# The last products of the PEER mixer, turned over: feature-major sums in PSUM in place of token-major ones

## The reference

```python
def chunk(args):
    xc, ec, gc = args
    ug = u[ec]
    act = jax.nn.gelu(jnp.einsum('td,thkd->thk', xc, ug), approximate=False)
    return jnp.einsum('thk,thkd->td', gc * act, v[ec])
...
x = x + (1.0 + gt2[:, None, :]) * peer_ffn(h, ...)
```

## Time and profile before

| | |
|---|---|
| median of 3 runs | 3288.6 us |
| the profiled execution | 3290.19 us, of which the span of its instructions is 3288.4 us |
| TensorE busy (matmul / weight load) | 90% / 81% of the span |
| VectorE, ScalarE, GpSimd busy | 70%, 34%, 3% |
| granted TensorE clock, mean | 0.954 of 2.4 GHz |
| scores stage of layer 0, layer 1 | about 808 to 1257.9, 2439 to 2890.1 us |
| mix stage of layer 0, layer 1 | about 1257.9 to 1620.5, 2890.1 to 3253.8 us |

### The profile page before, as it was taken

How to read it: one execution, slowest core, us unless ns; L and a number is a source line. 1 busy time by engine, 2 the same in 40 slices (tenths; PEclk the granted TensorE clock), 3 DMA queues, 4 the chain that set the end, 5 groups by cost and what they waited for, 6 DMA issues and landing times. The chain is left out here.

```text
span 3288.4 us, 49870 instructions
## 1 busy us (share of the span) xinstructions
PE 2962.9 (90%) x19180; PEld 2662.7 (81%) x19180; DVE 2314.4 (70%) x4571; ACT 1114.9 (34%) x1532; POOL 99.0 (3%) x120
## 2 busy tenths in 40 slices
PE   4997898879999999999769879897899999999996
PEld 4996787768999998887569858776789999988885
DVE  6888564545887847888578895645468868478885
ACT  3434321201444444333234342211024444433332
POOL 0000003200000000000000000031000000000000
PEclk8998999989999999999979989998999999999998
DMA  6552340053666688887465424300546575978783
GB/s 243 184 188 77 119 170 8 29 208 116 207 208 213 215 295 283 283 280 277 142 238 188 156 77 159 129 8 32 211 139 213 189 249 190 320 266 284 278 281 109
DMA packets 268992, 613.57 MB, mean 187 GB/s; under 512 B 45520, under 2 KB 210000, under 8 KB 211664
## 3 DMA queue, kind: packets, MB, share of 16 engines
q1 hardware_dynamic: 203152, 576.79, 49.9%
q10 hardware_dynamic: 65600, 33.55, 3.4%
HBM read 540.53 MB, written 69.73 MB: 186 GB/s over the span
## 5 line engine op out<-in xcount | busy, mean ns | idle before, releaser
L835 PE MATMUL ps<-h_hi,u_hi 128*128 128x256 f32 x2048 | 592.0, 289 | 34.6 <-DVE u_lo L1563 34.2
L835 PE MATMUL ps<-h_hi,u_lo 128*128 128x256 f32 x2048 | 582.4, 284 | 0.0
L835 PE MATMUL ps<-h_lo,u_hi 128*128 128x256 f32 x2048 | 582.2, 284 | 0.0
L1563 DVE TENSOR_TENSOR u_lo<-ring,u_hi 128x1024 fp32r<-128x1024 f32 x256 | 311.7, 1220 | 252.4 <-ACT u_hi L1067 251.9
L835 PEld LDWEIGHTS ps<-h_hi,u_hi 128*128 128x128 f32 x2048 | 395.5, 193 | 42.9 <-DVE u_lo L1563 36.0
L1075 ACT ACTIVATE v_hi<-ring 128x1024 fp32r<-128x1024 f32 x256 | 271.3, 1062 | 437.8 <-PE ps L856 437.8
L835 PEld LDWEIGHTS ps<-h_lo,u_hi 128*128 128x128 f32 x2048 | 395.5, 193 | 0.0
L835 PEld LDWEIGHTS ps<-h_hi,u_lo 128*128 128x128 f32 x2048 | 395.2, 193 | 0.0
L1570 DVE TENSOR_TENSOR v_lo<-ring,v_hi 128x1024 fp32r<-128x1024 f32 x256 | 313.1, 1224 | 49.3 <-ACT v_hi L1075 44.5
L856 PE MATMUL ps<-v_hi,w_hi 128*128 128x512 f32 x1024 | 323.5, 397 | 4.3 <-DVE w_lo L1682 4.3
L856 PE MATMUL ps<-v_lo,w_hi 128*128 128x512 f32 x1024 | 322.9, 396 | 0.0
(11 more groups left out here) (300 smaller groups left out, 4363.0 us busy)
## 6 DMA issues: line engine op xcount, KB each, us to landing
ring<-in_stream SPq DMA_DIRECT2D x444, 1024.0 KB, 5.0
act_rows<-region SPq DMA_DIRECT2D x256, 128.0 KB, 5.5
gate_rows<-region ACTq DMA_DIRECT2D x4, 8192.0 KB, 55.6
region<-gate_rows SPq DMA_DIRECT2D x256, 128.0 KB, 4.6
region<-act_rows SPq DMA_DIRECT2D x256, 128.0 KB, 4.7
region<-in_c SPq DMA_DIRECT2D x6, 512.0 KB, 3.6
xT<-in_x SPq DMA_DIRECT2D x1, 1024.0 KB, 7.9
small_inverses<-route SPq DMA_DIRECT2D x4, 256.0 KB, 2.0
```

Of the source, the lines that this page charges most:

```text
L835: ins = mm(ps[:, c % 4, 0:T], x, y[:, k, :], start=k == 0 and i == 0, stop=k == KD - 1 and i == 2)
L1563: vec.tensor_tensor(u_lo[:, c % U_DEEP, :], ring[:, slot, (c % 2) * D:(c % 2 + 1) * D], u_hi[:, c % U_DEEP, :].bitcast(F32), ALU.subtract) ...
```

## The change

In the mix, stationary and moving operand change places. The stationary operand is now a block of 128 experts x 128 features of `v_hi` or `v_lo`, the moving one the 256 tokens of `w_hi` or `w_lo`, and the sum that grows in PSUM is feature-major, two feature blocks to a bank. A chunk has 8 feature blocks x 3 parts, 24 matmuls of 256 columns. Since two sums share a bank, none of them is begun with `start`; four matmuls of a stationary block of zeros with 512 columns of constants set banks 4 to 7 to zero ahead of the first chunk, and four more close the sums behind the last. The zeros are a new tile, written once by VectorE at the kernel's start. The two copies to `acc`, the 16 transposes, `acc` itself and three semaphores go away; VectorE adds from banks 4 to 7. `acc_ready` now counts once.

```diff
+        zero = sb("zero", [P, P])
...
-                    for tt in range(TT):
-                        wh, wl = (w[:, c % 2, tt * P:(tt + 1) * P] for w in (w_hi, w_lo))
-                        for i, (x, y) in enumerate(((wh, v_hi), (wh, v_lo), (wl, v_hi))):
-                            for half in range(2):
-                                ins = mm(ps[:, 4 + 2 * tt + half, :], x, y[:, c % V_DEEP, half * 512:(half + 1) * 512],
-                                         start=c == 0 and i == 0, stop=c == CHUNKS - 1 and i == 2)
-                        if c == CHUNKS - 1:
-                            ins.then_inc(S["acc_ready"], 1)
-                    if c < CHUNKS - 1:
-                        ins.then_inc(S["mixed"], 1)
+                    for k in range(KD):
+                        vh, vl = (v[:, c % V_DEEP, k * P:(k + 1) * P] for v in (v_hi, v_lo))
+                        for x, y in ((vh, w_hi), (vh, w_lo), (vl, w_hi)):
+                            ins = mm(ps[:, 4 + k // 2, (k % 2) * T:(k % 2 + 1) * T], x, y[:, c % 2, :],
+                                     start=False, stop=False, skip_group_check=True)
+                    ins.then_inc(S["mixed"], 1)
...
                 pe.wait_ge(S["gates_copied"], STEPS)
+                for b in range(4):
+                    mm(ps[:, 4 + b, :], zero[:, :], K("pair_mask"), start=True, stop=False, skip_group_check=True)
                 for c in range(CHUNKS):
                     mix(c)
-                pe.wait_ge(S["acc_copied"], 1)
-                pe.wait_ge(S["rest_copied"], 1)
-                for tt in range(TT):
-                    for k in range(KD):
-                        ins = nc.tensor.transpose(ps[:, k // 2, k % 2 * T + tt * P:k % 2 * T + (tt + 1) * P], acc[:, tt, k * P:(k + 1) * P], ident)
-                ins.then_inc(S["acc_T"], 1)
+                for b in range(4):
+                    ins = mm(ps[:, 4 + b, :], zero[:, :], K("pair_mask"), start=False, stop=True, skip_group_check=True)
+                ins.then_inc(S["acc_ready"], 1)
...
-                act.wait_ge(S["acc_ready"], 1)
-                A(acc[:, 0, :], ps[:, 4:6, :].rearrange("p b n -> p (b n)"), ACT.Copy).then_inc(S["acc_copied"], 1)
...
+            vec.memset(zero[:, :], 0.0)
...
-                dve.wait_ge(S["acc_ready"], 2)
-                vec.tensor_copy(acc[:, 1, :], ps[:, 6:8, :].rearrange("p b n -> p (b n)")).then_inc(S["rest_copied"], 1)
-                dve.wait_ge(S["acc_T"], 1)
+                dve.wait_ge(S["acc_ready"], 1)
```

More of the change, by code:

```diff
@@ L307, in build @@
         w_hi, w_lo = over(hot_at, "w_hi", 512, 2, T), over(hot_at, "w_lo", 1024, 2, T)
-        acc = view(10240, TT, D)
         gates_dram = nc.dram_tensor("gate_rows", (KEYS, P, T), F32, kind="Internal").ap()
@@ L334, in build @@
                  "key_mm", "key_read", "route_T", "route_copied", "hot_ready", "gates_mm", "gates_copied", "s_ready", "s_gelu",
-                 "acc_ready", "acc_copied", "rest_copied", "acc_T", "red_mm", "kk_squares", "kk_sums", "kk_root", "kk_recip", "kk_spread", "bonus_mm", "pre_ready", "ar_ready", "gn_mm", "gn_root", "zeroed", "lam_sum", "lam_exp", "att_squares", "conv_act", "lora_act",
+                 "acc_ready", "red_mm", "kk_squares", "kk_sums", "kk_root", "kk_recip", "kk_spread", "bonus_mm", "pre_ready", "ar_ready", "gn_mm", "gn_root", "zeroed", "lam_sum", "lam_exp", "att_squares", "conv_act", "lora_act",
                  "gn_squares", "ln_squares", "bonus_prod", "rwkv_out", "merged_ready", "normed", "ln_affine", "decay_sums",
@@ L1701, in _ @@
                         weigh(c + 2)
-                dve.wait_ge(S["acc_ready"], 2)
-                vec.tensor_copy(acc[:, 1, :], ps[:, 6:8, :].rearrange("p b n -> p (b n)")).then_inc(S["rest_copied"], 1)
-                dve.wait_ge(S["acc_T"], 1)
+                dve.wait_ge(S["acc_ready"], 1)
                 for k in range(KD):
-                    ins = vec.scalar_tensor_tensor(xT[:, k, :], ps[:, k // 2, (k % 2) * T:(k % 2 + 1) * T], gate1[:, 1, k:k + 1],
+                    ins = vec.scalar_tensor_tensor(xT[:, k, :], ps[:, 4 + k // 2, (k % 2) * T:(k % 2 + 1) * T], gate1[:, 1, k:k + 1],
                                                    xT[:, k, :], ALU.mult, ALU.add)
```

## The result

The changed kernel took 3310.36 us (median of 4 runs, 3306.76 to 3319.42) against 3286.97 us (median of 4 runs) before. The ratio is 1.0069, with a 95% interval of 1.005 to 1.009: slower by 23 us in the medians, where +20.9 and 3309.5 us had been forecast. The profiled execution took 3312.06 us (span 3310.3), 21.9 more than the one before.

What follows compares the result with a forecast made beforehand. The mix was taken to last as long as TensorE's stream of matmuls, set by the spacing of starts. Terms 17.6 + 3.7 - 0.3 + 0.2 - 0.4 + 0.1 = +20.9 us on 3288.6 gave 3309.5 us, range 3298 to 3316.

Steps and rivals of the forecast that it cites:

- The stream: Mix matmuls: 24 of 256 columns at the scores' 0.1200 us make a chunk 2.880 for 2.811 us, +17.6 us.
- rival A: Mix: roles don't matter, only width; pace 0.1175 or 0.1171 us a matmul, about 3294 us; chance 0.09.
- The leading zero matmuls: Four ahead of each mix, two instructions each, 3.44 us, partly hidden by the wait at chunk 4; +3.7 us for both.
- The tail: Behind each mix: four closing matmuls replace copy and transposes, 3.65 us for 3.55; +0.2 us for both layers.
- The second gap: TensorE's gap of 1.08 us at 2932.63 shrinks by four times 0.069 us, -0.3 us.
- the semaphores: Three semaphores less to clear on the way into the next layer, 0.07 us each, -0.4 us.
- the zeros: Zeros written once ahead of VectorE's first instruction, between 0 and 0.29 us, taken as +0.1 us.
- C: Mix gets faster, 0.108 us a matmul and 2.592 us a chunk, 3236 us; chance 0.03.
- B: Mix: smaller fixed part, 3 ns per instruction, +9 us and 3.3 for the rest, 3301 us; chance 0.04.
- D: Mix: TensorE starves on weight loads or instruction fetch; twice the "issue" time +7 us, 3317 us and above; chance 0.06.

Runs made afterwards that it cites:

- e8: Changed kernel with the w_hi and w_lo buffers 16 bytes further apart and 32 bytes of padding ahead of w's tile; 3308.5 us in one run.
- e1: Kernel before, old roles kept, each mix matmul of 512 columns cut into two of 256; 3298.3 against 3287.3 us, ratio 1.0029.
- e3: Changed kernel with the four buffers of v_hi and of v_lo 16 bytes further apart, row buffers moved up; 3305.8 us in one run.
- e2: Changed kernel without zero matmuls and tile of zeros, start and stop flags on real matmuls instead; 3298.3 against 3287.3 us for the kernel before, ratio 1.0037.
- e4: Kernel before with 32 bytes of padding ahead of the tile of w_hi, w_lo and zh_hi; 3280.1 against 3287.3 us, ratio 0.9979.
- e5: Kernel before with the u_hi and u_lo buffers 16 bytes further apart and h_hi, h_lo, act_s moved up; 3285.5 us in one run.
- e7: Changed kernel with the two buffers of w_hi and of w_lo, the moving operand, 16 bytes further apart; 3310.3 us in one run.
- e6: e2 with every v_hi and v_lo buffer 16 bytes behind a multiple of 64; 3292.3 against 3280.9 us for the kernel before, ratio 1.0023.
- e10: Changed kernel with only the order within a chunk changed, 8 feature blocks for each operand pair in turn; 3304.3 us in one run.
- e9: Kernel before with 32 bytes of padding ahead of w and the u buffers 16 bytes further apart; 3275.2 against 3282.0 us, ratio 0.9975.
- e12: e2 with the v buffers of e3 and the u buffers of e5; 3280.7 against 3282.0 us for the kernel before, ratio 0.9998.

## Why the prediction was right, and where its reason was not

- *The stream, +17.6 us.* 256 chunks at 2.880 for 2.811: the size is exact. It was taken from a stage of the same form whose stationary blocks stand at multiples of 64 bytes as `v` does. That it fits to a thousandth is in part luck: the scores move `h` from multiples of 64, the mix moves `w` from 32 bytes behind one, and with `w_hi` and `w_lo` at a multiple of 64 the chunk takes 2.908 (e8, even chunks). The reason given, a fixed part of 0.006 us per instruction, was wrong for the most part. e1 has the width without the new roles and costs 0.006 to 0.036 a chunk; e3 has both and costs 0.004 to 0.018 over the old 2.811 in three chunks of four. The step that failed is the one that read "an fp32r matmul of half the width costs more than half" out of two stages that also differ in where their operands stand. The earlier trace rows had the warning: 0.1198 and 0.1175 at one width. I put that down to the roles (rival A), yet e1 with the old roles at half width runs at 0.117 and at 0.119.
- *The leading zero matmuls, +3.7 us.* Two instructions each, 3.44 us, less the wait at chunk 4: 3.4 measured (e2). The wait was bound by a load that doesn't hang on the mix, as the earlier trace rows said.
- *The tail, +0.2 us.* 3.63 for 3.55. The copies and transposes that went, and the four doubled matmuls that came, are worth the same; e2 shows what a tail without either is.
- *The second gap, -0.3, the semaphores, -0.4, the zeros, +0.1.* The gap of 1.08 us went whole, but layer 1 now has waits and late starts of 1.2 us at chunks 22, 80 and 116. The other two are below what two traces can tell. The new first instruction of VectorE is drawn with 0.17 us.
- *The rivals.* A and C fell at 0.1200 in line 855, and so did B, whose 0.003 us per instruction asks for 2.847 a chunk. B's price, 3301, is near e1's 3298, but it asks for one spacing, and e1 has two. D fell: "issue" at line 855 is 2.6 us, 6.9 before, though loads and matmuls doubled.

  The Trainium skill's rule ("TensorE: Matmul & The Clock Gate", section "Back-to-back issue gap", N/2.4 + 2.5 ns) stays below every fp32r spacing here: 109 ns for 256 columns against 117 to 121, 216 ns for 512 against 233 to 234. The page gives this rule for an isolated matmul and, for a steady stream of loads and matmuls, about 131 ns at 512 columns; the prediction had left that out, and no stream here comes near it.

Open is what the spacing follows. Shown is that it moves with the place of the operands (e3, e4, e5, e7, e8), with that of the moving one alone too (e7, e8), that it can take several values with nothing changed (e1, e6), changing behind a disturbance in e1 and in a fixed round in e6, and that the order of the parts doesn't matter (e10). A pattern in which TensorE's reads of the two operands fall in step with something would do this, but no run isolates it. No run takes away what the other engines and the DMA read and write beside it either; that scores and mix both held 2.880 beside different work speaks against it. Also open is how much of e1's excess is the width's own, and so how much the new form costs at the best places of both: 2.791 (e9) against 2.836 on average (e12, layer 0) is what was reached.

## What to carry to other kernels

A pace is best taken from a stage with the same form and the same placement, and a match without the latter is partly luck; an explanation taken from two stages needs the one edit that separates its causes. Where TensorE's stream is the bound, try the operands' buffers 16 or 32 bytes further on before anything is rewritten, and measure each try: it gave 0.2 to 0.25% here for one to four lines (e4, e9), and in e8 it made the chunks slower. And plain float32 matmuls that only set or close a sum are not free: count them twice, and let the start flag of the first real matmul do it.

## What the runs showed of the hardware

- fp32r matmuls at 2.4 GHz had spacings of 0.117 to 0.121 us at 256 columns and 0.2326 to 0.2343 at 512, by the place of their operands.
- The same stream with the same addresses ran at 2.817 and at 2.847 us a chunk, and changed from one to the other behind a wait of 0.32 us (e1).
- A plain float32 matmul of 512 columns is two instructions of 0.43 us each.
- A start flag on the first matmul into a bank was enough for two sums that share it: the second one, without a flag, began from zero (e1, e2).
